# One of the four weight sums of each K range on GpSimd instead of the Vector engine

## The reference

```python
def swiglu(h, w_gate, w_up, w_down):
    return (jax.nn.silu(h @ w_gate) * (h @ w_up)) @ w_down

# in each of the two layers
x = x + mix
h = rms_norm(x, ffn_norm[layer])
x = x + swiglu(h, ffn_w_gate[layer], ffn_w_up[layer], ffn_w_down[layer])
```

## Time and profile before

| what | value |
|---|---|
| median of 3 runs | 1935.91 us |
| the profiled execution's own time | 1935.77 us |
| its span | 1934.0 us |
| mean granted TensorE clock | 0.999 |
| Vector engine busy | 1401.7 us (72%), 1049 instructions |
| ScalarE busy | 929.7 us (48%) |
| GpSimd busy | 23.7 us (1%), 85 instructions |
| sums of L1009 | 64 instructions, 144.9 us |
| read from HBM | 377.53 MB |

### The profile page before, as it was taken

One profiled execution on the slowest core, in us unless ns is written; L12 is line 12 of the kernel. 1 busy time (PEld: TensorE's weight loads), 2 busy tenths in 40 slices (PEclk: granted clock), 3 DMA queues, 4 the chain that ended last, 5 costly groups with the idle time before them and its releaser, 6 DMA issues.

```text
span 1934.0 us, 21993 instructions
## 1 busy us (share of the span) xinstructions
PE 1920.5 (99%) x9272; PEld 1611.1 (83%) x9272; DVE 1401.7 (72%) x1049; ACT 929.7 (48%) x728; POOL 23.7 (1%) x85
## 2 busy tenths in 40 slices
PE   9999999999999999999999999999999999999998
PEld 7889999988888888888888888888888888888886
DVE  6656788855757868878778556756878868968755
ACT  6444434436434545545445445733544544645443
POOL 1000000000000000000000030000000000000000
PEclk9999999999999999999999999999999999999999
DMA  9554444455555654747666655464675765746762
GB/s 311 179 176 162 153 152 152 151 177 164 183 196 193 242 196 174 270 143 246 236 204 232 226 184 174 145 203 152 209 269 183 252 199 194 261 134 239 258 211 93
DMA packets 214874, 380.92 MB, mean 197 GB/s; under 512 B 5937, under 2 KB 55170, under 8 KB 214530
## 3 DMA queue, kind: packets, MB, share of 16 engines
q1 hardware_dynamic: 214560, 379.10, 58.0%
q10 hardware_dynamic: 226, 0.55, 0.1%
HBM read 377.53 MB, written 2.10 MB: 196 GB/s over the span
## 4 chain that ended last, share of the span: by engine, by line
PE 87%; DVE 9%; ACT 1%; DMA 1%; issue 1%; SPq 0%; DVEq 0%; ACTq 0%
PE main L1620 38%; PE main L1626 19%; PE main L1562 8%; PE aux L1642 5%; DVE lo L1003 5%; PE main L1564 4%; DVE raw L1009 4%; PE aux L1646 2%; PE main L1642 2%; PE aux L1569 2%; PE main L1646 2%; PE aux L1731 1%; ACT hi L641 1%; PE main L1673 1%; PE main L1675 1%
## 5 line engine op out<-in xcount | busy, mean ns | idle before, releaser
L641 ACT CAST hi<-raw 128x2048 fp32r<-128x2048 f32 (+1 forms) x389 | 741.7, 1907 | 776.3 <-PE main L1626 494.4
L1003 DVE TENSOR_TENSOR lo<-raw,hi 128x2048 fp32r<-128x2048 f32 x316 | 719.7, 2290 | 320.8 <-ACT hi L641 320.5
L1620 PE MATMUL main<-hi,act 128*128 128x512 f32 x1968 | 468.4, 390 | 0.0
L1620 PEld LDWEIGHTS main<-hi,act 128*128 128x128 f32 x1968 | 368.0, 188 | 76.0 <-DVE act L1302 0.3
L1620 PE MATMUL main<-hi,mid 128*128 128x512 f32 x1616 | 385.8, 391 | 0.5 <-DVE mid L1270 0.5
L1620 PEld LDWEIGHTS main<-hi,mid 128*128 128x128 f32 x1616 | 301.7, 188 | 64.1 <-DVE mid L1270 1.6
L1626 PE MATMUL main<-lo,act 128*128 128x512 f32 x984 | 243.1, 389 | 0.0
L1562 PE MATMUL main<-act,hi 128*128 128x512 f32 x640 | 229.1, 401 | 0.0
L994 DVE TENSOR_TENSOR lo<-raw,hi 128x2048 fp32r<-128x2048 f32 x71 | 162.6, 2290 | 79.5 <-ACT hi L641 79.5
L1626 PEld LDWEIGHTS main<-lo,act 128*128 128x128 f32 x984 | 184.7, 188 | 38.3
L1626 PE MATMUL main<-lo,mid 128*128 128x512 f32 x808 | 199.6, 389 | 0.0
(11 more groups left out here) (186 smaller groups left out, 1338.4 us busy)
## 6 DMA issues: line engine op xcount, KB each, us to landing
raw<-in_ffn_w_gate SPq DMA_DIRECT2D x104, 1024.0 KB, 5.2
raw<-in_ffn_w_up SPq DMA_DIRECT2D x88, 1024.0 KB, 6.3
raw<-in_ffn_w_down SPq DMA_DIRECT2D x88, 1024.0 KB, 5.1
raw<-in_ab_w_in SPq DMA_DIRECT2D x55, 1024.0 KB, 5.1
raw<-in_ab_w_out SPq DMA_DIRECT2D x16, 1024.0 KB, 5.0
raw<-in_pool_w SPq DMA_DIRECT2D x4, 1024.0 KB, 5.5
xn<-in_x SPq DMA_DIRECT2D x4, 512.0 KB, 8.3
raw<-in_ab_w_in SPq DMA_DIRECT2D x2, 512.0 KB, 6.3
```

Source lines behind the costliest of these rows:

```text
L641: return nc.scalar.copy(out_, in_)
L1003: V.tensor_tensor(lo[:, split_at(t), :], src, hi[:, split_at(t), :].bitcast(F32), ALU.subtract).then_inc(lo_ready, 1)
L1620: mm(o2[:, h, :], lhs[:, k0 + n, c, h * P:(h + 1) * P], w_hi, start=(first and c == 0 and n == 0), stop=False)
```

## The change

Sum (1,2), b12 + b22 for slot 4, leaves the Vector engine and goes to GpSimd, with a semaphore of its own (`pool_sum`). GpSimd starts it when sum (0,1), which reads b12, is made and b22 is loaded. ScalarE waits for it ahead of the copy of slot 4. The place of b22 is given back for a new transfer when lo 2 is made, as before, and now also when the GpSimd sum has been made. The Vector engine's wait for b22 moves behind lo 1. The other three sums keep their order.

```diff
-BLOCK, BLOCK_SUMS = 6, 4
+BLOCK, BLOCK_SUMS = 6, 3
...
-            free += [(b22.at, s + 3), (b11.at, s + 4), (b12.at, s + 5), (b21.at, s + 6)]
+            pooled += 1
+            free += [(b22.at, s + 3, pooled), (b11.at, s + 4, 0), (b12.at, s + 5, 0), (b21.at, s + 6, 0)]
...
-SUM_FOR = {1: 1, 3: 3, 4: 2, 5: 4}
+SUM_FOR = {1: 1, 3: 2, 5: 3}
+POOL_SUM_FOR = 4
...
             def place(p, src):
 
                 sp.wait_ge(lo_ready, p.free)
+                if p.pooled:
+                    sp.wait_ge(pool_sum, p.pooled)
                 sp.dma_start(raw[:, p.at, :].rearrange("p (k c) -> p k c", k=4), src).then_inc(raw_loaded[p.at], 16)
...
+            def sum_blocks(g):
+
+                for s0 in g.blocks:
+                    n = block_index(s0)
+                    b11, b12, b22, b21 = PLACES[s0]
+                    pool.wait_ge(raw_loaded[b22.at], 16 * b22.lap)
+                    pool.wait_ge(sum_made, BLOCK_SUMS * n + 1)
+                    nc.gpsimd.tensor_tensor(raw[:, b12.at, :], raw[:, b12.at, :], raw[:, b22.at, :], ALU.add
+                                            ).then_inc(pool_sum, 1)
+
+            for g in LAYERS[0]:
+                sum_blocks(g)
             pool.wait_ge(job_emptied, LAYERS[0][-1].j_down)
             pool.wait_ge(slot_used, LAYERS[0][-1].x + 2)
...
+            for g in LAYERS[1]:
+                sum_blocks(g)
...
                     if i in SUM_FOR:
                         sc.wait_ge(sum_made, BLOCK_SUMS * block_index(s0) + SUM_FOR[i])
+                    elif i == POOL_SUM_FOR:
+                        sc.wait_ge(pool_sum, block_index(s0) + 1)
...
                 if i == 0:
                     loaded(1)
                     add(0, 1)
+                if i == 1:
                     loaded(2)
-                    add(1, 2)
-                if i == 1:
                     add(0, 2)
                 if i == 2:
                     loaded(3)
-                    ve.wait_ge(sum_made, BLOCK_SUMS * block_index(s0) + 3)
+                    ve.wait_ge(sum_made, BLOCK_SUMS * block_index(s0) + 2)
                     add(3, 0)
```

More of the change, by code:

```diff
@@ L153 @@
     lap: int
+    pooled: int = 0
 def places():
-    free = [(s % RING, s + 1) for s in range(S_FFN0 - RING, S_FFN0)]
-    laps, out, s = [S_FFN0 // RING] * RING, {}, S_FFN0
+    free = [(s % RING, s + 1, 0) for s in range(S_FFN0 - RING, S_FFN0)]
+    laps, out, s, pooled = [S_FFN0 // RING] * RING, {}, S_FFN0, 0
     def take():
-        at, lo = free.pop(0)
+        at, lo, count = free.pop(0)
         laps[at] += 1
-        return Place(at, lo, laps[at])
+        return Place(at, lo, laps[at], count)
     while s < SLOTS:
@@ L172, in places @@
             out[s] = [take()]
-            free.append((out[s][0].at, s + 1))
+            free.append((out[s][0].at, s + 1, 0))
             s += 1
@@ L452, in trunk @@
         sum_made = sem("sum_made")
+        pool_sum = sem("pool_sum")
         x_copied = sem("x_copied")
```

## The result

The changed kernel takes 1967.84 us (median of 5 runs, 1966.75 to 1968.44) against 1935.22 before. The ratio is 1.0167 with a 95% interval of 1.0156 to 1.0179: 1.7% slower, 32.6 us. The forecast was 1966.

The account below looks back on a forecast made before the run. TensorE, busy 1920.5 of 1934.0 us, was taken as the bound, with at most 6.7 us from relieving DVE. First-block losses of 19.1 and second-block losses of 11.4 made 30.5 us on 1935.77: 1966.3, range 1947 to 1982.

Parts of the forecast that it names:

- What the removed sum was worth: Sum (1,2) on DVE lies almost wholly beside ScalarE's copy of slot 1; removing it wins 1.2 us, not 35.
- What the added sum costs by itself: GpSimd's sum of 2048 columns takes 4.6 us, 0.18 of it fixed; as work of its own it is hidden.
- What it costs DVE: GpSimd, always first, delays lo 1; TensorE loses 2.39 us in each first block and 1.42 in each second.
- the hold: DVE's two-SBUF-input instruction stands still while GpSimd's sum runs; lo 1 was forecast to end 2.15 us behind GpSimd.
- The sum: Total over 16 blocks: 8 x 2.39 + 8 x 1.42 = 30.5 us, giving 1966.3 us, 1.6% slower.
- Three of the signs that were named: Trace signs: GpSimd starts within 0.1 of sum (0,1)'s end; TensorE's `lo` waits about 37 us, newly in first blocks' slot 2.
- (a): Rival: a running GpSimd sum doesn't hold the interface; lo 1 starts at 601.22, 1.2 us won, 1934.6; chance 0.11.
- its break-even point: In (a): lo 1 ends no later than before if GpSimd's sum takes at most 2.23 us.
- (b): Rival: lo 1 runs at half speed while GpSimd finishes, DVE losing about 1.3; 11 us, 1947; chance 0.05.
- (c): Rival: GpSimd gives way whenever DVE asks, delaying slot 4's copy; 3.0 us a block, 49 in all, 1985; chance 0.06.
- (d): Rival: as forecast, but GpSimd's sum takes 7.4 us; 74 us, 2010; chance 0.04.

Follow-up runs that it names:

- kernel without the sum: Changed kernel without its GpSimd instruction and the two waits for it, so nobody makes sum (1,2): 1934.52 us, ratio 0.9997.
- kernel with writes alone: Changed kernel with GpSimd writing zeros over tile b12 for about 4.6 us in place of the sum, reading no SBUF: 1934.17 us, ratio 0.9992.
- half sum: Changed kernel with GpSimd adding only the first 1024 of 2048 columns: 1937.55 us, ratio 1.0013.
- kernel with quarters: Changed kernel with the same sum in four GpSimd instructions of 512 columns: 1961.27 us, ratio 1.0136.

## Why the prediction was right

- **What the removed sum was worth:** 1.2 us was predicted by the cover of ScalarE's copy. The kernel without the sum stands 0.8 us below the one before, within its uncertainty; lo 1 moved by the 0.15 us that was named.
- **What the added sum costs by itself:** 4.62 us predicted, 4.617 measured. Half the columns took 2.41, a quarter that had to wait for nobody 1.28: that is 0.28 us for 128 columns and 0.2 fixed, the two parts that were assumed, so the agreement isn't luck. Its SyncE and ScalarE waits cost nothing, as the kernel with writes alone shows.
- **What it costs DVE:** the hold stood on one row of 0.13 us for the direction that mattered. It is shown now in both: DVE is held until 2.14 or 2.15 us ahead of its own end by a sum of 2.41 and of 4.61 us, and GpSimd behind DVE grew from 4.62 to 6.54. That GpSimd must read is shown by the kernel with writes alone; that DVE's instruction must have both inputs in SBUF, by the residual add's unchanged 1.21. Turns, and not sharing, is shown by the lengths: the one that is first keeps its usual time.
- **The sum:** 30.5 us predicted, 32.6 measured. The largest part of the difference is the start of GpSimd: 0.15 us behind sum (0,1) (600.69 against 598.25 + 2.29 = 600.54), where I took ScalarE's 0.03. That is 0.12 x 16 = 1.9 us. With it lo 1 is 2.5 us late in both kinds of block, and TensorE's losses are 2.51 and 1.54 instead of 2.39 and 1.42: 8 x 2.51 + 8 x 1.54 = 32.4 us. Three of the signs that were named came out a little off: GpSimd starts 0.15 behind sum (0,1) and not within 0.1; TensorE's weight loads wait 40.9 us in all and not about 37; and there is a short wait of 0.19 for lo 2 in second blocks too, where none was forecast.
- **The rivals:** (a), no contention, fell with the long record of lo 1, though its break-even point held: at 2.41 us instead of 2.23 the loss was 2 us. (b), shared speed, fell with the changed kernel itself: lo 1 grew by 2.64 us and not by 1.3, and GpSimd's sum wasn't slowed: its 4.62 us are less than four times the 1.28 us of a quarter that ran alone. The half sum (2 us and not 16) speaks only against a cost in proportion to GpSimd's work, which (b) was not. (c), GpSimd giving way, fell with GpSimd's steady 4.6 and with the quarters that came in between. (d) fell with the duration.
- **One thing that the forecast did not ask:** whether anything was to be won by other means. It said at most 6.7 us, and 6 were found by moving work that does not touch GpSimd.

## What to carry to other kernels

Before moving a two-input elementwise operation from DVE to GpSimd, count its reading time on GpSimd (here 4.6 us for 128x2048 in float32, twice DVE's 2.29) as time in which DVE can't run another operation with two SBUF inputs, and look for idle DVE time or one-input work of that length beside it. Where there is too little, the move can cost more than it takes away: with 1.8 us of it this kernel lost 33 us, with 1.1 us 52. And look first at what the removed work was worth; here it lay beside ScalarE's copy and was worth about 1 us or nothing. DVE was only a few tenths of a microsecond late ahead of TensorE, and moving other work behind the late instruction served better here (6 us); when doing so, check that no buffer comes back later, in each kind of neighbour that the pattern has.

## What the runs showed of the hardware

- A waiting GpSimd instruction gets its turn between two DVE instructions that stand back to back in the queue (3.38 us records of 2.29 us work, in the kernel with quarters).
- The hold ends before the record does: DVE's instruction ends 2.15 us behind GpSimd's record though it takes 2.29 when nothing holds it, so by this difference it is let in about 0.14 us before that end (an estimate from the records, and the profile's spans of GpSimd are rough).
- By their records GpSimd starts 0.12 us later on the same semaphore than ScalarE does (600.69 and 600.57), and 0.09 us later for a memset (600.53 against 600.44 in the kernel with writes alone).
